# A two-block transformer step on one core: forget-gate chain, second convolution, bias rows and the feed-forward's first wait moved

## What is computed

```
first block:
  hn   = rms_norm(x);  proj = hn @ w_in          # q, k, v, forget gate (8 cols), rx, rg
  q, k = rms_norm per head (8 heads of 128)
  c    = cumsum(log_sigmoid(proj_f * rstd + b_forget))
  att  = softmax(q.k/sqrt(128) + c_t - c_s, causal) @ v
  rx   = causal conv, 4 taps (8 tiles of 128 channels)
  rnn  = gelu(rg) * rg_lru(rx)                    # two gates by 8 block-diagonal matmuls, then a scan
  h    = x + concat(att, rnn) @ w_out
  h   += mixture of 32 experts (top 1 group, top 2 experts)
  h   += sigmoid(rms_norm(h) @ w_ple_gate) * (p @ w_ple_up)
second block:
  h   += 16 self-attention heads with relative bias rows from a table, @ w_out_2
  h   += cross attention to 256 memory rows
  gu   = rms_norm(h) @ w_up_2                     # 2 x 5632 columns
  h   += (silu(conv3(g)) * u) @ w_down_2          # contraction over 5632 = 44 tiles of 128
  out  = rms_norm(h)
```

## Time and profile before

| | |
|---|---|
| median of 3 runs | 2335.27 us (2334.82 to 2345.84) |
| profiled execution, its own time | 2340.84 us |
| its span | 2339.0 us |
| TensorE busy | 2242.4 us (96%) |
| VectorE busy | 1315.8 us (56%) |
| ScalarE busy | 894.8 us (38%) |
| GpSimd busy | 25.8 us (1%) |
| mean granted TensorE clock | 0.986 |
| DMA | 519.38 MB, mean 222 GB/s |

### The profile page before, as it was taken

One profiled execution on the slowest core, in us unless ns is written; L12 is line 12 of the kernel. 1 busy time (PEld: TensorE's weight loads), 2 busy tenths in 40 slices (PEclk: granted clock), 3 DMA queues, 4 the chain that ended last, 5 costly groups with the idle time before them and its releaser, 6 DMA issues.

```text
span 2339.0 us, 30793 instructions
## 1 busy us (share of the span) xinstructions
PE 2242.4 (96%) x11459; PEld 1692.4 (72%) x11459; DVE 1315.8 (56%) x1757; ACT 894.8 (38%) x1197; POOL 25.8 (1%) x32
## 2 busy tenths in 40 slices
PE   9999898899999999899999999979999999999997
PEld 8786777644444443678888878868888888878886
DVE  7795465422222222656666755647777777764443
ACT  4652354311111111535445444435343443433332
POOL 1000000000000000000000000000000000000000
PEclk9999999899999999899999999999999999999999
DMA  8654455499999999456555455535665565555653
GB/s 289 185 164 132 120 180 203 177 383 410 398 410 408 407 408 409 142 190 216 175 168 171 155 161 184 178 107 165 186 188 183 185 188 184 184 188 192 195 192 123
DMA packets 301293, 519.38 MB, mean 222 GB/s; under 512 B 24032, under 2 KB 196096, under 8 KB 292224
## 3 DMA queue, kind: packets, MB, share of 16 engines
q1 hardware_dynamic: 298272, 505.51, 62.5%
q0 software_dynamic: 2912, 12.38, 1.5%
HBM read 515.67 MB, written 5.27 MB: 223 GB/s over the span
## 4 chain that ended last, share of the span: by engine, by line
PE 88%; DVE 7%; ACT 2%; issue 1%; DMA 1%; POOL 0%; DVEq 0%; SPq 0%; ACTq 0%; POOLq 0%
PE acc L649 29%; PE acc L669 23%; PE acc L670 12%; PE ps L1039 9%; PE acc L1061 5%; PE tp L989 3%; PE tp L1001 2%; DVE wlo L1699 2%; PE tp L1002 1%; PE tp L733 1%; PE ps L803 1%; DMA raw<-in_w_in 1%; DVE h L2238 1%; DMA mw<-in_w_expert_up 1%; PE tp L817 1%
## 5 line engine op out<-in xcount | busy, mean ns | idle before, releaser
L669 PE MATMUL acc<-xhl,whi 128*128 128x512 f32 x2496 | 894.2, 402 | 12.9 <-DVE wlo L1699 4.1
L1699 DVE TENSOR_TENSOR wlo<-raw,whi 128x1024 fp32r<-128x1024 f32 x572 | 674.6, 1221 | 221.2 <-ACT whi L1271 217.7
L1271 ACT ACTIVATE whi<-raw 128x1024 fp32r<-128x1024 f32 x572 | 582.3, 1054 | 411.4 <-DMA raw<-in_w_down 141.7
L670 PE MATMUL acc<-xhl,wlo 128*128 128x256 f32 x2496 | 701.9, 281 | 0.0
L669 PEld LDWEIGHTS acc<-xhl,whi 128*128 128x128 f32 x2496 | 471.4, 189 | 130.6 <-issue 6.3
L670 PEld LDWEIGHTS acc<-xhl,wlo 128*128 128x128 f32 x2496 | 473.8, 190 | 0.9 <-issue 0.5
L649 PE MATMUL acc<-whi,xhl 128*128 128x512 f32 x800 | 258.8, 398 | 2.0 <-DVE xhl L1768 1.1
L1039 PE MATMUL ps<-mw,xg 128*64 128x512 f32 x1024 | 229.8, 595 | 2.1 <-DMA mw<-in_w_expert_up 1.3
L2238 DVE TENSOR_TENSOR h<-tp,h 128x512 f32<-128x512 f32 x128 | 87.6, 690 | 172.7 <-PE tp L1002 172.3
L649 PEld LDWEIGHTS acc<-whi,xhl 128*128 128x128 f32 x800 | 152.0, 190 | 42.0 <-issue 6.4
L1039 PEld LDWEIGHTS ps<-mw,xg 128*64 128x64 f32 x1024 | 70.8, 137 | 141.0 <-issue 137.6
(11 more groups left out here) (362 smaller groups left out, 2153.6 us busy)
## 6 DMA issues: line engine op xcount, KB each, us to landing
raw<-in_w_in SPq DMA_DIRECT2D x352, 256.0 KB, 3.0
raw<-in_w_up SPq DMA_DIRECT2D x352, 256.0 KB, 2.9
mw<-in_w_expert_gate SPq DMA_DIRECT2D x128, 512.0 KB, 8.2
mw<-in_w_expert_up SPq DMA_DIRECT2D x128, 512.0 KB, 9.3
mw<-in_w_expert_down SPq DMA_DIRECT2D x64, 1024.0 KB, 12.1
raw<-in_w_down SPq DMA_DIRECT2D x176, 256.0 KB, 3.3
raw<-in_w_out SPq DMA_DIRECT2D x128, 256.0 KB, 3.3
raw<-in_w_ple_gate SPq DMA_DIRECT2D x64, 256.0 KB, 3.6
```

What stands on the lines that cost most here:

```text
L669: pe.matmul(o.rearrange("p (m n) -> p m n", m=2), wh, ahl[:, :, k, :], start=first, stop=False, skip_group_check=True)
L670: return pe.matmul(o[:, S:2 * S], wl, ahl[:, 0, k, :], start=False, stop=last, skip_group_check=True)
L1271: act.activation(whi[:, m % RING, :], raw[:, m % RING, :], ACT.Copy).then_inc(hi_ready, 1)
L1699: dve.tensor_tensor(wlo[:, m % RING, :], raw[:, m % RING, :], whi[:, m % RING, :], ALU.subtract).then_inc(lo_ready, 1)
```

## The change

It has four parts.

1. TensorE no longer waits for all 22 rounds of the hidden row before the down projection; in the first of the four blocks, chunk c waits for round c+1 alone.
2. VectorE's forget-gate chain and ScalarE's exponential in it come before the root and the reciprocal of the q/k norm.
3. VectorE's `consume(4)` (chunks 20 to 23) comes before `conv(1)`.
4. On the GpSimd queue, the wait for `frev` and its write stand ahead of the gate weights, `f_raw`, `negsel` and `causal`; the 3 MB write of `skew_d` is issued after the gate matmuls and the router load.

```
--- before.py
+++ after.py
@@ -529,6 +529,8 @@
             pool.dma_start(onehot[:, :], I["onehot"]).then_inc(small_in, 16)
             pool.dma_start(addend[:, :], I["addend"]).then_inc(small_in, 16)
             pool.dma_start(iscale[:, :], I["iscale"]).then_inc(small_in, 16)
+            pool.wait_ge(b_f, 1)
+            pool.dma_start(frev_d, frev[:, :]).then_inc(b_out, 16)
             pool.dma_start(w_rec[:, :, :], I["w_rec_gate"][0].rearrange("n i j -> i n j")).then_inc(gates_in, 16)
             pool.dma_start(w_ing[:, :, :], I["w_in_gate"][0].rearrange("n i j -> i n j")).then_inc(gates_in, 16)
             pool.wait_ge(consts, 1)
@@ -536,14 +538,12 @@
             pool.dma_start(negsel[:, :, :], I["negsel"]).then_inc(late_in, 16)
             pool.dma_start(causal[:, :], I["causal"]).then_inc(late_in, 16)
 
-            pool.wait_ge(b_f, 1)
-            pool.dma_start(frev_d, frev[:, :]).then_inc(b_out, 16)
-            pool.wait_ge(b_out, 16)
-            pool.dma_start(skew_d, frev_d.rearrange("u (a m) -> u a m", a=1).broadcast_to((N_SELF, P, 384))).then_inc(b_rows, 16)
 
             pool.wait_ge(gate_mm, RNN_T)
             pool.memset(rt_raw[:, KT * N_ROUTER:], 0.0).then_inc(rt_pad, 1)
             pool.dma_start(rt_raw[:, 0:KT * N_ROUTER], I["w_router"]).then_inc(rt_in, 16)
+            pool.wait_ge(b_out, 16)
+            pool.dma_start(skew_d, frev_d.rearrange("u (a m) -> u a m", a=1).broadcast_to((N_SELF, P, 384))).then_inc(b_rows, 16)
 
             pool.wait_ge(o_lo, HEADS1)
             pool.wait_ge(rnn_lo, 2)
@@ -1240,14 +1240,14 @@
                     features(xhl)
                 n.leave(FF_T // 4 - 1)
                 bl.leave(FF_T // 4 - 1)
-            pe.wait_ge(a_lo, FF_T // 2)
 
             def ff(k):
                 if k < FA:
                     return ah[:, k, :], al[:, k, :]
                 return xh[:, k - FA, :], xl[:, k - FA, :]
 
-            for _ in range(4):
+            tokens(ff, FF_T // 2, lambda c: pe.wait_ge(a_lo, c + 1))
+            for _ in range(3):
                 tokens(ff, FF_T // 2)
             assert n.n == N_CHUNKS
 
@@ -1435,13 +1435,13 @@
             squares(3)
 
             consume(4)
+            act.wait_ge(f_abs, 1)
+            act.activation(z_y[:, :], z_n[:, :], ACT.Exp, scale=-1.0).then_inc(f_y, 1)
             act.wait_ge(ms_mm, 1)
             act.activation(inv[:, :], ps[0][0:8, :], ACT.Sqrt, bias=eps[0:8, 0:1]).then_inc(ms_root, 1)
             consume(1)
             act.wait_ge(inv_ready, 1)
             act.activation(inv_h[:, :], inv[:, :], ACT.Copy).then_inc(inv_hi, 1)
-            act.wait_ge(f_abs, 1)
-            act.activation(z_y[:, :], z_n[:, :], ACT.Exp, scale=-1.0).then_inc(f_y, 1)
             consume(11)
             bl.n += 2
 
@@ -1935,9 +1935,9 @@
             for c in (4, 6):
                 consume(4)
                 from_rows(rxp[:, c:c + 2, 4:4 + S])
+            consume(4)
             conv(1)
 
-            consume(4)
             dve.tensor_scalar(qg[:, 0:1], col(V_QN), HEAD_SCALE, None, ALU.mult)
             own(dve.tensor_scalar(qg[:, 1:2], col(V_SUB), 1.0 - LAM_INIT, None, ALU.mult))
             dve.wait_ge(lam_e, 2)
@@ -2024,25 +2024,25 @@
                 bl.n += 1
 
             consume(4)
+            dve.wait_ge(f_done, 1)
+            own(dve.tensor_tensor(z_f[:, :], tp[0][0:8, 0:S], rowR[0:8, :], ALU.mult))
+            mine()
+            own(dve.tensor_scalar(z_f[:, :], z_f[:, :], vec[0:8, V_BF:V_BF + 1], None, ALU.add))
+            mine()
+            own(dve.tensor_scalar(z_n[:, :], z_f[:, :], -1.0, None, ALU.mult))
+            mine()
+            dve.tensor_tensor(z_n[:, :], z_n[:, :], z_f[:, :], ALU.max).then_inc(f_abs, 1)
+            dve.wait_ge(f_y, 1)
+            own(dve.memset(z_1[:, :], 1.0))
+            log1p(z_y[:, :], z_z[:, :], z_q[:, :], z_s[:, :], z_n[:, :])
+            own(dve.scalar_tensor_tensor(z_f[:, :], z_f[:, :], 0.0, z_n[:, :], ALU.min, ALU.subtract))
+            mine()
+            dve.tensor_tensor_scan(c_cum[0:8, :], z_1[:, :], z_f[:, :], 0.0, ALU.mult, ALU.add).then_inc(c_ready, 1)
             dve.wait_ge(ms_root, 1)
             dve.reciprocal(inv[:, :], inv[:, :]).then_inc(inv_ready, 1)
             consume(1)
             dve.wait_ge(inv_hi, 1)
             dve.tensor_tensor(inv_l[:, :], inv[:, :], inv_h[:, :], ALU.subtract).then_inc(inv_lo, 1)
-            dve.wait_ge(f_done, 1)
-            own(dve.tensor_tensor(z_f[:, :], tp[0][0:8, 0:S], rowR[0:8, :], ALU.mult))
-            mine()
-            own(dve.tensor_scalar(z_f[:, :], z_f[:, :], vec[0:8, V_BF:V_BF + 1], None, ALU.add))
-            mine()
-            own(dve.tensor_scalar(z_n[:, :], z_f[:, :], -1.0, None, ALU.mult))
-            mine()
-            dve.tensor_tensor(z_n[:, :], z_n[:, :], z_f[:, :], ALU.max).then_inc(f_abs, 1)
-            dve.wait_ge(f_y, 1)
-            own(dve.memset(z_1[:, :], 1.0))
-            log1p(z_y[:, :], z_z[:, :], z_q[:, :], z_s[:, :], z_n[:, :])
-            own(dve.scalar_tensor_tensor(z_f[:, :], z_f[:, :], 0.0, z_n[:, :], ALU.min, ALU.subtract))
-            mine()
-            dve.tensor_tensor_scan(c_cum[0:8, :], z_1[:, :], z_f[:, :], 0.0, ALU.mult, ALU.add).then_inc(c_ready, 1)
             consume(1)
             for i, g in enumerate(QK_ORDER):
                 consume(1)
```

More of the change, by code:

```diff
@@ L537, in _ @@
             pool.dma_start(causal[:, :], I["causal"]).then_inc(late_in, 16)
[L539 to L542, removed]
             pool.wait_ge(gate_mm, RNN_T)
@@ L2026, in _ @@
             consume(4)
[L2027 to L2031, removed]
             dve.wait_ge(f_done, 1)
@@ L2045, in _ @@
             dve.tensor_tensor_scan(c_cum[0:8, :], z_1[:, :], z_f[:, :], 0.0, ALU.mult, ALU.add).then_inc(c_ready, 1)
+            dve.wait_ge(ms_root, 1)
+            dve.reciprocal(inv[:, :], inv[:, :]).then_inc(inv_ready, 1)
+            consume(1)
+            dve.wait_ge(inv_hi, 1)
+            dve.tensor_tensor(inv_l[:, :], inv[:, :], inv_h[:, :], ALU.subtract).then_inc(inv_lo, 1)
             consume(1)
```

## The result

| | before | changed |
|---|---|---|
| median of 16 executions | 2342.11 us | 2322.05 us |
| profiled execution, its own time | 2340.84 us | 2325.31 us |
| its span | 2339.0 us | 2323.5 us |

The account below looks back on a forecast made before the run. TensorE, busy 96% of the span, was taken as the bound, so only its idle or slow time could be won. Terms 3.36 + 5.09 + 6.05 - 1.3 = 13.2 us off 2335.27 gave 2322.1 us; range 2316 to 2330.

Parts of the forecast that it names:

- Chunk 20, gain 3.36: Before the gates, TensorE's 3.36 us idle time ahead of chunk 20 was to vanish entirely.
- both causes go: Before chunk 20: splits move ahead of the convolution and the 3 MB write no longer delays loads; 3.36 us gained.
- The write in its new place, loss 1.3: After the gates, the 3 MB write delays loads and VectorE, so TensorE waits 1.3 us before chunk 44.
- The forget chain, gain 5.1: Third spread: chain fills VectorE's idle time, removing 3.71 us wait and 1.58 us slow clock, less 0.2 us wait.
- The down projection, gain 6.05: Start of the down projection: 4.33 us idle time and 1.72 us of slow clock behind it were to go.
- The sum: Whole kernel: gains 3.36, 5.09 and 6.05 less a loss of 1.3 make 13.2 us, time 2322.1.
- the hidden write: After the gates, the 3 MB write costs nothing and VectorE keeps its lead: 14.7 us gained, time 2320.6; chance 0.2.
- The late chain: Forget-gate chain makes TensorE wait at the first spread instead of the third: 8.1 us gained, time 2327.2; chance 0.1.
- the costly write: After the gates, the write makes TensorE wait 5.3 us before chunk 44: 7.6 gained, time 2327.7; chance 0.18.
- The starved ring: After the gates, the write delays chunk 32's load, costing 17 us: time 2337.6; chance 0.07, shared with a failing part.
- rule of turns: After the gates, DMA engines alternate between queues packet by packet: chunk 32 lands near 107, loss about 0.3 us.

## Why the prediction was right, and where it was not

- *Chunk 20, gain 3.36:* right, no idle time is left and the stretch is 4.4 us shorter, 1.0 of it from the quicker pace, which is chance (in the other traces without an idle time there it is 45.3 us or more, not 44.5). That "both causes go" was right too, but I did not say that one would do: either part alone is enough.
- *The write in its new place, loss 1.3:* the term that was mis-sized. The delays were as worked out (chunk 32 landed by 111.85 against 111.5, chunk 35 by 116.1 against 117.2), VectorE's scan came 1.4 us later and not 2.6, and TensorE's pace from chunk 24 was the slow one, 2.83 us and not the 2.77 of the earlier trace rows. So chunk 44 had 0.7 us to spare where I had it 1.3 short. At the quick pace the wait was 0.53 us in one trace and none in two others. The term is 0 to 0.5. A part of the miss is thus the pace, which I took as fixed; had it been 2.77 in the first trace, chunk 44 would have been wanted about 1 us earlier and would have waited about 0.3 us (an estimate).
- *The forget chain, gain 5.1:* 5.36 measured, 5.3 by undoing it. The 0.2 us of wait at the first spread did not come, since VectorE was 1.2 us less late; `inv_l` was ready 0.4 to 1.8 us before that spread in the traces that have both the chain and the write in their new places.
- *The down projection, gain 6.05:* 6.1 by undoing it.
- *The sum:* 15.0 instead of 13.2, so the middle of the interval (17.1) is 2.1 us above the sum of the steps, and its low end (13.6) lies under it. The 1.8 us that 13.2 lacks of 15.0 are 1.3 of the write's term, 0.3 of the spread's and 0.15 of the down projection's.
- *The rivals:* the hidden write (14.7 us) came nearest to what happened, though not by its reason, for VectorE did lose its lead, 4.0 of 4.7 us. The late chain and the costly write did not happen. The starved ring did not happen with one write; two in a row bring it, for 8 to 9 us and not 17. The prediction's estimate by the Trainium skill's rule of turns (DMA: Bandwidth & Descriptors, Queues, rings and completion order) had put the loss at 0.3 by an earlier chunk 32; it came at 111.85 and no earlier than by the measured delays, and the loss was small because VectorE was less late behind it.
- *What I left out:* the spells of slow clock elsewhere, 1.7 us each or a multiple of it, and the two paces. The gain behind the two removed idle times (1.6 and 1.7) was in the sum. Between the changed kernel's two traces the clock's lack differs by 5.3 us, and the pace changes the up projection's stretch by 7.4 us; single executions spread over 20 us, and what the ones without a trace did can't be read.

## What to carry to other kernels

On an in-order engine, give the one that stalls its work first (a split, a chain with a waiting reader) and let the side work fill the idle time behind it; and when two edits cure one wait, undo each by itself, for one of them may only spend the lead that the next stretch needs. Where TensorE waits for about 2 us or more, count with a slow clock behind it that may cost 1.7 us more; it did not always come here. Matmuls on a constant, timed to stop short of the wait's end, kept the clock at 1.00 at five places (some 6 us of 2324, not clear of the spread), and too many of them cost 18 us.

## What the runs showed of the hardware

- Behind idle times of 3.7 and 4.3 us TensorE's granted clock fell to about 0.5, the lower of its two levels (1.2 GHz), and a spell cost 1.6 to 1.8 us. Behind one and the same idle time of 2.11 us (up projection, second block) it fell in four of the ten traces without fills and not in the other six. Behind the 3.36 us of the earlier trace rows it did not fall, and behind 2.56 us at the same place (parts 3 and 4 undone) it did.
- The same matmuls at the same granted clock of 1.00 ran 1.9% apart (0.347 and 0.353 us), by stretch and by execution.
- A 3 MB write from HBM to HBM took 15.1 to 17.7 us beside the chunk loads, over all traces; a second behind it landed 26.2 us after its issue, 11 us after the first. Loads queued beside a write came late: chunk 32, asked for 2 us behind it, took about 15 us where others took 3, and with the second write chunk 33 came 9 us behind chunk 32 where it came 1.4 behind with one.
